# Gate projections of the odd mixer and of the hybrid mixer's third branch: three 256-column products against a 512 + 256 pair, with the gate functions one step later

## The reference, cut to what matters

```python
def odd_mixer(h, w_in, out_norm, w_out, pos):
    ...
    g = z[..., 2 * nq + nv:]                       # 2048 gate columns of h @ w_in
    o = rmsnorm(retention(q, k, v), out_norm)
    o = o.reshape(B, S, nv).astype(h.dtype) * jax.nn.silu(g)
    return o @ w_out

def hybrid_mixer(x, ...):
    ...
    gates = jax.nn.sigmoid(x @ w_gate + b_gate).reshape(b, t, N_BRANCH, d)
    merged = (gates[:, :, 0] * (o_a @ w_br_a) + gates[:, :, 1] * (o_b @ w_br_b)
              + gates[:, :, 2] * (o_c @ w_br_c))
    return merged @ w_out
```

## Time and profile before

| | |
|---|---|
| median of 3 runs | 2330.03 us (2330.02 to 2330.04) |
| the profiled execution, its own time | 2329.93 us |
| its span | 2328.1 us |
| TensorE matmul busy | 2308.4 us, 99% |
| VectorE busy | 1782.5 us, 77% |
| ScalarE busy | 1282.7 us, 55% |
| GpSimd busy | 79.9 us, 3% |
| mean granted TensorE clock | 0.999 |

### The profile page before, as it was taken

How to read it: one execution, slowest core, us unless ns; L and a number is a source line. 1 busy time by engine, 2 the same in 40 slices (tenths; PEclk the granted TensorE clock), 3 DMA queues, 4 the chain that set the end, 5 groups by cost and what they waited for, 6 DMA issues and landing times.

```text
span 2328.1 us, 37280 instructions
## 1 busy us (share of the span) xinstructions
PE 2308.4 (99%) x14968; PEld 2093.2 (90%) x14968; DVE 1782.5 (77%) x2694; ACT 1282.7 (55%) x2001; POOL 79.9 (3%) x96
## 2 busy tenths in 40 slices
PE   8999999999999999999999999999999999999998
PEld 7988889998888888999999888888889999998887
DVE  6989657779758876797679886698767976798854
ACT  6855444655535544585556554455545855565542
POOL 0022000002100000020000000000000200000000
PEclk9999999999999999999999999999999999999999
DMA  6456564455556555553355555556565543456563
GB/s 228 136 190 192 188 208 165 144 163 208 179 176 211 188 188 189 196 178 126 120 172 180 192 190 181 172 191 202 185 191 194 177 135 118 156 177 220 190 184 106
DMA packets 115451, 412.43 MB, mean 177 GB/s; under 512 B 12880, under 2 KB 14800, under 8 KB 115024
## 3 DMA queue, kind: packets, MB, share of 16 engines
q1 hardware_dynamic: 114992, 407.96, 53.3%
q0 software_dynamic: 288, 2.10, 0.3%
HBM read 408.96 MB, written 1.05 MB: 176 GB/s over the span
## 4 chain that ended last, share of the span: by engine, by line
PE 94%; DVE 4%; ACT 1%; issue 1%; DMA 0%; SPq 0%; DVEq 0%; ACTq 0%
PE ps L435 93%; DVE wlo L1927 1%; PE ps L710 0%; DMA raw<-in_ew_c 0%; ACT whi L1193 0%; DVE xx L2149 0%; DVE x L2142 0%; DVE RX L2113 0%; DVE x L1979 0%; ACT region L1394 0%; DVE x L2120 0%; PE ps L941 0%; PE ps L1018 0%; DVE x L2078 0%; DVE H L1950 0%
## 5 line engine op out<-in xcount | busy, mean ns | idle before, releaser
L435 PE MATMUL ps<-xx,whi 128*128 128x512 f32 (+1 forms) x4632 | 1224.7, 351 | 3.2 <-DVE xx L1987 1.6
L1927 DVE TENSOR_TENSOR wlo<-raw,whi 128x1024 fp32r<-128x1024 f32 (+3 forms) x772 | 927.0, 1208 | 275.0 <-ACT whi L1193 273.8
L1193 ACT ACTIVATE whi<-raw 128x1024 fp32r<-128x1024 f32 (+3 forms) x772 | 801.4, 1044 | 562.1 <-PE ps L435 548.4
L435 PE MATMUL ps<-xx,wlo 128*128 128x256 f32 x3696 | 807.7, 279 | 0.0
L435 PEld LDWEIGHTS ps<-xx,wlo 128*128 128x128 f32 x3696 | 697.2, 189 | 121.6
L435 PEld LDWEIGHTS ps<-xx,whi 128*128 128x128 f32 x4632 | 717.7, 190 | 8.9 <-issue 3.8
L435 PE MATMUL ps<-H,whi 128*128 128x512 f32 (+1 forms) x2144 | 547.5, 343 | 2.2 <-DVE H L1950 2.2
L435 PE MATMUL ps<-H,wlo 128*128 128x256 f32 x1632 | 364.8, 279 | 0.0
L435 PEld LDWEIGHTS ps<-H,wlo 128*128 128x128 f32 x1632 | 308.3, 189 | 50.4
L435 PEld LDWEIGHTS ps<-H,whi 128*128 128x128 f32 x2144 | 333.2, 190 | 3.6 <-DVE H L1950 2.8
L1922 DVE TENSOR_REDUCE t<-ps 128x256 f32<-128x512 f32 x320 | 219.8, 688 | 46.5 <-PE ps L435 39.8
(11 more groups left out here) (300 smaller groups left out, 1569.0 us busy)
## 6 DMA issues: line engine op xcount, KB each, us to landing
raw<-in_sg SPq DMA_DIRECT2D x128, 512.0 KB, 3.6
raw<-in_su SPq DMA_DIRECT2D x128, 512.0 KB, 3.6
raw<-in_sd SPq DMA_DIRECT2D x128, 512.0 KB, 3.9
raw<-in_mw_g SPq DMA_DIRECT2D x48, 512.0 KB, 3.6
raw<-in_fg SPq DMA_DIRECT2D x44, 512.0 KB, 3.3
raw<-in_fu SPq DMA_DIRECT2D x44, 512.0 KB, 3.3
raw<-in_fd SPq DMA_DIRECT2D x32, 512.0 KB, 3.5
raw<-in_mw_a SPq DMA_DIRECT2D x24, 512.0 KB, 3.7
```

The costliest lines, as they stand in the source:

```text
L435: return e.matmul(out, lhsT, rhs, start=start, stop=stop, skip_group_check=True)
L1193: e.activation(m.whi[:, c % NHL, 0:cw], m.raw[:, c % NRAW, 0:cw], ACT.Copy).then_inc(s["whi"].h, s["whi"].up(c))
L1927: e.tensor_tensor(m.wlo[:, c % NHL, 0:cw], m.raw[:, c % NRAW, 0:cw], m.whi[:, c % NHL, 0:cw].bitcast(F32), ALU.subtract).then_inc(s["wlo"] ...
```

## The change

The 16 chunks of the odd mixer's gates and the 8 chunks of the hybrid's third branch in each layer, 32 in all, go through `gemm_wide`. In the odd mixer VectorE adds the halves of the bank, GpSimd multiplies by `R`, and ScalarE applies Silu to gate i-1 where it did gate i. In the hybrid each chunk has a whole bank, chunk i of a pair in bank i; VectorE gets a sum of halves per chunk (`last_sum`) and ScalarE applies Sigmoid from SBUF, a pair later (`last_gates`).

```diff
 # TensorE, odd
-            gemm_fm("ow_g", i, take(i % 4, ("rdve", "g", i))[:, 0:256], xh, xl)
+            gemm_wide("ow_g", i, take(i % 4, ("rdve", "g", i)))
...
 # TensorE, hybrid
         for p in range(4):
-            gates(2, p, take(p % 2, ("gate", l, 2, p)))
+            for i in range(2):
+                gemm_wide(f"mw_g{l}", 16 + 2 * p + i, take(i, ("gsum", l, 2, p, i)))
+                side.step()
...
 # ScalarE, odd
+        def gate(i):
+            w.wait_ge(s["rpool"], i)
+            e.activation(m.sg[:, i, :], m.sg[:, i, :], ACT.Silu).then_inc(s["ract"].h, s["ract"].up("g", i))
         for i in range(16):
             chunk()
-            w.wait_ge(s["rdve"], "g", i)
-            e.activation(m.sg[:, i, :], m.sg[:, i, :], ACT.Silu).then_inc(s["ract"].h, s["ract"].up("g", i))
+            if i:
+                gate(i - 1)
...
 # ScalarE, hybrid
+        def last_gates(p):
+            for i in range(2):
+                w.wait_ge(s["gsum"], l, 2, p, i)
+                t = e.activation(m.mgs[p][:, i, :], m.mgs[p][:, i, :], ACT.Sigmoid, bias=pk(f"bg{l}", 16 + 2 * p + i))
+            t.then_inc(s["gate"].h, s["gate"].up(l, 2, p))
+
         for p in range(4):
-            gates(2, p, p % 2, m.mgs[p])
+            chunk()
+            if p:
+                last_gates(p - 1)
+            side.step()
+            chunk()
+            side.step()
...
 # VectorE, odd
-            e.tensor_tensor(m.sg[:, i, :], ps[i % 4][:, 0:256], R[:, 0, :], ALU.mult).then_inc(
-                s["rdve"].h, s["rdve"].up("g", i))
+            both(m.sg[:, i, :], ps[i % 4]).then_inc(s["rdve"].h, s["rdve"].up("g", i))
...
 # VectorE, hybrid
+        def last_sum(p, i):
+            w.wait_ge(s["gemm"], f"mw_g{l}", 16 + 2 * p + i)
+            halves_sum(m.mgs[p][:, i, :], ps[i]).then_inc(s["gsum"].h, s["gsum"].up(l, 2, p, i))
+
         side.step()
         chunk()
         chunk()
+        last_sum(0, 0)
         side.step()
         for p in range(1, 4):
-            gates()
+            chunk()
+            last_sum(p - 1, 1)
+            side.step()
+            chunk()
+            last_sum(p, 0)
+            side.step()
         side.until(lambda: "C" in flag)
         for p in range(4):
             chunk()
+            if p == 0:
+                last_sum(3, 1)
             side.step()
...
 # GpSimd
+    def gates():
+        w.wait_ge(s["rstd"], "o")
+        for i in range(16):
+            g = m.sg[:, i, :]
+            w.wait_ge(s["rdve"], "g", i)
+            e.tensor_tensor(g, g, m.R[:, 0, :], ALU.mult).then_inc(s["rpool"].h, s["rpool"].up(i))
```

More of the change, by code:

```diff
@@ L394 @@
     "rdve",
+    "rpool",
     "pact",
@@ L1610, in odd @@
             chunk()
+            if c == 0:
+                gate(15)
             if c == 4:
@@ L1841, in hybrid @@
             chunk()
+            if p == 0:
+                last_gates(3)
             side.step()
@@ L3075, in gpsimd_program @@
     norm("f0", 22)
+    gates()
     norm("f1", 22)
```

## The result

The changed kernel takes 2343.24 us (2342.64 to 2343.99) against 2330.06 us (2330.02 to 2330.37) of the kernel before, a ratio of 1.0056, 95% interval 1.0047 to 1.0066: slower by 13.2 us. The forecast was 2339.7, in a range of 2336.6 to 2343.0: the direction and the place of the main loss were right, its size was not. The profiled execution took 2343.36 us, its span is 2341.6 us.

The account below looks back on a forecast made before the run. TensorE was taken to bound the kernel, its matmuls busy for 99% of the span. 2329.93 - 1.44 (odd mixer) + 9.66 (hybrid bank wait) = 2338.15 us; with 1.5 us for the clock 2339.7 us, range 2336.6 to 2343.0.

Parts of the forecast that it names:

- TensorE's clock: Hybrid: the clock may drop to half in the long pauses; chance six in ten, 0.75 us a layer, 1.5 us in all.
- Shorter chunks: All 32 changed gate chunks: each takes 2.79 us instead of 2.88, saving 0.09; the odd mixer's 16 give -1.44 us.
- Odd mixer's VectorE, GpSimd and ScalarE work at 0: Odd mixer gates: longer VectorE sums (0.69 for 0.42 us) and 16 GpSimd multiplies of 1.22 us fit in slack; priced 0.
- It has time: Odd mixer: VectorE can absorb the longer sums, since it waited 3.95 us before such a multiply.
- A bank has three more chunks, over 8 us: Odd mixer: three more chunks, over 8 us, pass before TensorE wants a gate's PSUM bank again.
- The bank wait in the hybrid: Hybrid gate chunk 2 waits for VectorE's sum of chunk 0, +5.46 us; net +4.83 a layer, +9.66 for both.
- the 9.66 us: Hybrid, both layers: bank wait and restart, less the transposes' vanished wait and what chunks 2 to 7 save.
- ScalarE in the hybrid: Hybrid: Sigmoid waits for chunk 1's sum, but copied attention weights still come in time; price 0, slack over 2 us.
- the bound: Hybrid: the most a clock drop can cost a stall, 4.8 / 2 = 2.4 us, from slow matmuls at the start.
- The first: Rival: no bank stall in the hybrid, all 32 chunks save 0.09 us; 2327.0 us, chance 0.05.
- The second: Rival: the hybrid's stall delays ScalarE, causing a second stall of some 2 us a layer; 2343.7 us, chance 0.05.
- The third: Rival: GpSimd's multiply in the odd mixer holds ScalarE, about 3.6 us more; 2343.3 us, chance 0.03.

Follow-up runs that it names:

- e7: Only the odd mixer changed, with its gate chunks 12 to 15 as in the kernel before; 2328.98 us, ratio 0.9995 to the kernel before.
- e4: Only the hybrid changed, with its first pair of gate chunks as in the kernel before; 2329.47 us, ratio 0.9997 to the kernel before.
- e1: The odd mixer's half of the change alone, hybrid as in the kernel before; 2329.74 us, ratio 0.9999 to the kernel before.
- e6: As e1, but GpSimd's 16 products with `R` left out, so gates lack the norm factor; 2329.02 us, ratio 0.9996 to the kernel before.
- e2: The hybrid's half of the change alone, odd mixer as in the kernel before; 2343.34 us, ratio 1.0057 to the kernel before.
- e3: As e2, but the sums of gate chunks 0 and 1 stand earlier in VectorE's queue; 2333.07 us, ratio 1.0013 to the kernel before.
- e5: As e2, with 22 matmuls into an unread bank ahead of gate chunk 2 in each layer; 2339.47 us, ratio 1.0041 to the kernel before.
- e9: As e1, but VectorE, not GpSimd, multiplies by `R` for gate chunks 12 to 15; 2330.64 us, ratio 1.0002 to the kernel before.

## Why the prediction was right or wrong

Two terms of the sum failed: the work of VectorE and GpSimd in the odd mixer, priced at 0, cost 1.22 us, and TensorE's clock, priced at 1.5 us, cost 4.06. The range allowed 4.8 us for the clock, so it is the first of them that carries the time out of it.

*Shorter chunks: right.* The rows' 0.09 us each held in the odd mixer to 0.01, 1.33 us over 16 chunks and 1.03 over 12 (e7), against the 0.3 us estimated for the 16 from the Trainium skill's page "TensorE: Matmul & The Clock Gate" (section Back-to-back issue gap). Behind side work in the hybrid it was less in e4.

*Odd mixer's VectorE, GpSimd and ScalarE work at 0: wrong.* This step failed: "It has time: before such a multiply it waited 3.95 us". That row is from 401.71, an early chunk. At the last four chunks VectorE has attention normalisation of the retention heads beside the gates and works without a pause. The kernel before had a margin of only 0.25 us there, as two rows of its timelines show: the last product ends at 444.91, and the second of the two matmuls at 445.04, which starts at 445.16, is the first that needs bank 3.

```profile
444.50 0.41 DVE L2638 TENSOR_TENSOR region<-ps,R 128x256 f32<-128x256 f32 x1
...
445.04 0.40 PE L435 MATMUL ps<-H,whi 128*128 128x256 f32 x2
```

In the changed kernel VectorE's last stretch (432.23 to 444.82, before 433.26 to 444.91) is longer by four sums in place of products (4 x 0.27 us) and by the 0.76 us that GpSimd's products cost it, and shorter by a wait for ScalarE of 0.79 us. That is 1.05 us more by these parts and 0.94 by the rows. It starts 1.0 us sooner, so it ends about when it did, while TensorE, 1.3 us ahead, wants the bank 1.3 us sooner. "A bank has three more chunks, over 8 us" was also wrong at the end: behind the gates bank 3 is wanted 2.1 us after the start of the output chunk. The odd mixer as a whole was to give -1.44 us and measured -0.22 in the changed kernel's rows and -0.3 in e1. e6 and e7 show the cause of the pause: without GpSimd's products the lost time falls from 1.11 to 0.35 us, without the last four sums and the products behind them to nothing.

*The bank wait in the hybrid: right to the hundredth.* Counted from the start of gate chunk 0 the restart was forecast at 11.22 us (1079.14 - 1067.92) and came at 11.21 in both layers (1079.10 - 1067.89 and 1905.54 - 1894.33); there is no pause ahead of chunk 3, and the small wait of chunk 1 shows in chunk 0's 2.89 us. That 1079.10 agrees with 1079.14 in absolute time is luck: the forecast took over the start of the kernel before, as if the odd mixer's forecast gain of 1.44 us were not there, and hardly any of it was. e2, e3 and e5 bear out the cause and the 9.66 us: e5, at full clock, is 9.5 us above the kernel before.

*ScalarE in the hybrid: right.* It waited for the sums and held up nothing.

*TensorE's clock: the mechanism right, the size wrong.* The fall came in every one of the four long pauses that were traced, two in the changed kernel and two in e2. The step that failed is "I give the drop six chances in ten and take half of the bound where it comes", 0.75 us a layer. It measured 1.34 and 2.72 us in the changed kernel, and 2.82 and 1.95 in e2 against e5. The bound itself, 2.4 us a layer, was also too low, by 0.4: it was taken from slow transposes at the start of the program, where the clock column prints 1.00, so no row shows that they are a rise of the clock. The row for the fall, 3.45 us behind the last matmul, lay 2 us inside the pause that the same prediction had just worked out, and spoke for a chance well above six in ten. A drop in both layers at the changed kernel's mean of 2.0 us would have given 2338.15 + 4.1 = 2342.2 us.

*Rivals.* The first (no stall, 2327.0) is refuted by the pauses. The second (ScalarE, 2343.7) came close to the time for no reason of its own: there is no second pause in either layer. The third named the right suspect, GpSimd in the odd mixer, and the wrong victim: it slowed VectorE, not ScalarE, and cost TensorE something only at the end.

## What to carry to other kernels

When an engine with a backlog gets a new piece of work on which TensorE's next bank hangs, count from its queue when it reaches that piece: here 5.5 us late, as the queue said. Read the slack of the last repetitions of a loop and not of a middle one, since what follows may take its buffers at another pace. And a pause of TensorE costs its own length and the lower clock behind it, here a quarter to a half more. Work moved to another engine may still cost the first one time: here about half of it.

## What the runs showed of the hardware

*GpSimd and VectorE.* Operations of VectorE with two inputs in SBUF are held up beside GpSimd's product: 0.74 for 0.43 us and 1.20 for 0.75 us (two operations), in all 0.76 us over the three products ahead of the last sum. The RECIPROCAL beside the first of them, with one input, took the same 1.74 us as in the kernel before. GpSimd's own product of 128x256 took 0.64 us beside that RECIPROCAL and up to 1.55 us beside a `wlo` chunk. The page "SBUF — State Buffer" of the Trainium skill (section "SBUF: two separate sides") says that a VectorE operation with two SBUF inputs and a GpSimd operation that reads SBUF exclude each other for the whole instruction, whichever starts first. The trace agrees, but for 0.15 us. Line 2635, which also reads two tiles in SBUF, starts at 438.07, ahead of GpSimd's product at 438.23: it keeps its 0.48 us, and the product takes 0.81. Line 2639 at 438.58 starts while the product runs, until 439.04, and ends at 439.32. In these rows the second of the two ends its own length less 0.15 us behind the end of the first (439.04 + 0.43 - 0.15 = 439.32; a `wlo` chunk's end at 445.96 + 0.64 - 0.15 = 446.45, the end of the product that took 1.55).

*TensorE's clock.* Behind 5.65 us between starts the clock was at half (1.2 GHz) when the matmuls began again, in all four cases. It had fallen 2.7 to 4.8 us behind the end of the last matmul and rose 3.4 us (changed kernel, layer 0) or 6.8 us (its layer 1, both layers of e2) behind the fall; the price was 1.34 to 2.82 us, each time 0.46 of the time that it was still at half behind the restart (2.94, 5.94, 6.15 and 4.28 us). The odd mixer's pauses, 1.15 us between starts in e1 and 1.56 in e9, left it at full (1.00 in both windows of the output chunk). Behind the long pause a chunk that runs wholly at half clock takes 5.28 us and not 2.79.
